# Upward products of a dense layer: high and low part of x in one product of 512 columns, with both sums left in PSUM for other engines to add

## The chip, the cores and the metric

The kernel runs on one core of one Trainium2 chip. The metric is the device time of the whole program in microseconds (us), the median of several runs. The engines are TensorE (PE, with its weight loads as PEld), VectorE (DVE), ScalarE (ACT), GpSimd (POOL) and SyncE (SP), which only issues transfers here.

## What is computed

The reference chains two transformer blocks over 256 positions of width 1024, all in float32. What the change touches are the three dense feed-forward parts:

```python
def swiglu(h, w1, w3, w2):                      # first block, D_FF = 2816
    return (jax.nn.silu(h @ w1) * (h @ w3)) @ w2
...
for l in range(DEPTH):                          # second block, two layers
    mod = c_act @ w_ada[l] + b_ada[l]
    ...
    h = rmsnorm(x, norm_mlp_g[l]) * (1.0 + sc2) + sh2
    x = x + g2 * (jnp.square(jax.nn.relu(h @ w_up[l])) @ w_down[l])   # w_up: 1024 x 4096
```

## The kernel before

**Split operands.** A float32 product is made of three products of rounded parts: with w = w_hi + w_lo and x = x_hi + x_lo it adds w_hi·x_hi, w_hi·x_lo and w_lo·x_hi (function `product`, lines 563 to 565). x is split once per stage. The weights stream from memory in slots of 128x2048 into a ring of six buffers; each slot is two halves of 128x1024. For every half ACT rounds it into `w_hi` (line 2321) and DVE subtracts to get `w_lo` (line 1416). There are three buffers of `w_hi`/`w_lo`, so a half can be rounded only when PE has finished the half three before it.

**Order.** All engines run written-out, in-order programs. `split_to(m)` on ACT and on DVE works off the splits up to half m; `reach(n)` is the number of halves that can be split once PE has finished n of them, which is n + 3 here. What stands behind a `split_to` waits in the same queue.

**Upward and downward products.** A step j makes 256 (of 2816 or 4096) hidden features. An upward half is 8 steps of k, each with three matmuls of 256 columns (`feature_tile`): w_hi, w_lo stand as weights and x moves. Two upward halves of one slot share one PSUM bank (256 columns each). The FFN needs two such slots in a step (w1, "gate", and w3, "up"), so four upward halves, called u0 to u3 below; the MLP needs one slot, u0 and u1. The downward product of the step before follows, two halves d0 and d1, each 12 matmuls of 512 columns. PE thus runs u0, u1, (u2, u3,) d0, d1 and again u0. The FFN has J1 = 11 steps, each of the two MLPs J2 = 16.

**The hidden values.** When the upward halves of step j are done, ACT applies Silu or Relu from PSUM into `ff` (line 2497), DVE multiplies (line 1663), rounds to `h_hi` (1427) and subtracts to `h_lo` (1428). The downward product of step j waits for that, one step of upward products later; after the last step there is no such upward work between, only one downward half and the first third of a group.

**Folds.** The slots of w_ada are streamed between the slots of the FFN and of the first MLP (layer 0), 24 in each. DVE takes each in whole, in two instructions (lines 1394 and 1402; the first 16 by the one, the last 8 by the other), in `split_to` right ahead of the first half of the slot that it is hung to. By `stream_order` the FFN has a fold ahead of each slot from its fifth to its last, except the slots 8, 13, 18, 23 and 28 (slot 0 is the first); the first MLP has one ahead of each from slot 4 to 31 except 8, 14, 20 and 26. The second MLP has none. In the FFN the first slot of step j is slot 3j-1, in the MLP 2j-1, so a fold stands ahead of u0 in 7 steps of the FFN (slots 5, 11, 14, 17, 20, 26, 29) and in 13 steps of the first MLP (all odd slots from 5 to 29).

## Time and profile before

| | before |
|---|---|
| median of 3 runs | 1919.96 us (1919.83 to 1922.27) |
| the profiled execution, first to last instruction | 1919.5 us |
| PE / PEld busy | 97% / 84% |
| DVE / ACT busy | 80% / 63% |
| granted TensorE clock, mean | 0.991 |
| FFN stage, 132 to 328 us | DVE 158.6 of 195.5 us busy |
| first MLP, 1395 to 1583 us | DVE 167.9 of 188.0 us busy |
| second MLP, 1728 to 1910 us | DVE 109.9 of 182.0 us busy |

The profile is one execution taken by the hardware profiler. The profiled execution's own time is its span, 1919.5 us from the first to the last instruction, 0.5 us under the median of the runs. Matmuls are pipelined, so their speed is read from the distance between two starts, not from the length of one.

### The profile page before, as it was taken

The numbers are of one execution on the slowest core, as the hardware profiler recorded it, in microseconds if no ns is written. First come the engines' busy times: TensorE is split into PE (matmuls) and PEld (weight loads), VectorE is DVE, ScalarE is ACT, GpSimd is POOL, SyncE is SP. The second block draws the span as 40 slices with busy tenths as digits, with TensorE's granted clock in tenths as the row PEclk, the third lists the DMA queues.
The fourth block names the chain that finished last, engine by engine and source line by source line (L and its number), as shares of the span: only waits on it lengthen the run. The fifth ranks groups of instructions, "written<-read, shape, count | busy, mean of one in ns | idle before, by whom it ended". The sixth has DMA issues, their size and how long they took to land.

```text
span 1919.5 us, 27067 instructions
## 1 busy us (share of the span) xinstructions
PE 1855.8 (97%) x10592; PEld 1606.9 (84%) x10592; DVE 1527.7 (80%) x2097; ACT 1200.0 (63%) x1650; POOL 46.1 (2%) x56
## 2 busy tenths in 40 slices
PE   8999999999999999999999999899999999999998
PEld 7889998788888888888888887688789988878997
DVE  5768887568999999999999999667589985756565
ACT  4544444646888888888888887567454446744443
POOL 0010000002000000000000010000000000000000
PEclk9999999999999999999999999999999999999999
DMA  8348896755999999999999999343278974315451
GB/s 317 132 165 307 329 346 245 279 203 218 420 389 377 383 377 390 369 391 375 396 368 388 367 403 380 145 154 129 69 272 332 356 278 154 129 70 187 181 192 44
DMA packets 76060, 528.37 MB, mean 275 GB/s; under 512 B 8690, under 2 KB 9074, under 8 KB 14610
## 3 DMA queue, kind: packets, MB, share of 16 engines
q1 hardware_dynamic: 69696, 504.40, 68.4%
q10 hardware_dynamic: 3060, 11.02, 1.6%
q0 software_dynamic: 3168, 11.14, 1.4%
q8 instruction: 86, 1.41, 0.3%
q14 instruction: 50, 0.41, 0.1%
HBM read 515.90 MB, written 11.01 MB: 275 GB/s over the span
## 4 chain that ended last, share of the span: by engine, by line
PE 88%; DVE 5%; ACT 3%; issue 2%; POOL 0%; DMA 0%; POOLq 0%; DVEq 0%; SPq 0%; ACTq 0%
PE ps L563 27%; PE ps L565 27%; PE ps L564 27%; PE ps L793 2%; PE ps L745 1%; DVE w_lo L1416 1%; PE ps L1015 1%; PE ps L758 1%; ACT w_hi L2321 1%; DVE arena L1402 1%; PE ps L580 0%; ACT score L2447 0%; POOL stat L2854 0%; ACT xT L2331 0%; PE ps L998 0%
## 5 line engine op out<-in xcount | busy, mean ns | idle before, releaser
L2321 ACT ACTIVATE w_hi<-ring 128x1024 fp32r<-128x1024 f32 x862 | 911.3, 1061 | 561.7 <-PE ps L565 551.9
L1416 DVE TENSOR_TENSOR w_lo<-ring,w_hi 128x1024 fp32r<-128x1024 f32 x862 | 1040.7, 1222 | 237.2 <-ACT w_hi L2321 224.2
L563 PE MATMUL ps<-w_hi,x_hi 128*128 128x512 f32 (+1 forms) x1056 | 409.5, 390 | 3.7 <-DVE x_lo L2011 1.4
L565 PE MATMUL ps<-w_hi,x_lo 128*128 128x512 f32 (+1 forms) x1056 | 399.7, 381 | 0.0
L564 PE MATMUL ps<-w_lo,x_hi 128*128 128x512 f32 (+1 forms) x1056 | 398.4, 380 | 0.0
L563 PE MATMUL ps<-x_hi,w_hi 128*128 128x256 f32 x1248 | 358.1, 287 | 8.4 <-DVE x_lo L1523 6.1
L564 PE MATMUL ps<-x_lo,w_hi 128*128 128x256 f32 x1248 | 353.7, 283 | 0.0
L565 PE MATMUL ps<-x_hi,w_lo 128*128 128x256 f32 x1248 | 353.6, 283 | 0.0
L563 PE MATMUL ps<-w_hi,h_hi 128*128 128x512 f32 x732 | 285.5, 390 | 2.7 <-DVE h_lo L1428 1.8
L564 PE MATMUL ps<-w_lo,h_hi 128*128 128x512 f32 x732 | 284.9, 389 | 0.0
L565 PE MATMUL ps<-w_hi,h_lo 128*128 128x512 f32 x732 | 284.3, 388 | 0.0
L563 PEld LDWEIGHTS ps<-x_hi,w_hi 128*128 128x128 f32 x1248 | 239.9, 192 | 14.2 <-DVE x_lo L1523 6.6
L564 PEld LDWEIGHTS ps<-x_lo,w_hi 128*128 128x128 f32 x1248 | 240.1, 192 | 1.4
L565 PEld LDWEIGHTS ps<-x_hi,w_lo 128*128 128x128 f32 x1248 | 239.9, 192 | 0.0
L563 PEld LDWEIGHTS ps<-w_hi,x_hi 128*128 128x128 f32 (+1 forms) x1056 | 192.4, 182 | 42.4 <-issue 2.5
L565 PEld LDWEIGHTS ps<-w_hi,x_lo 128*128 128x128 f32 (+1 forms) x1056 | 192.3, 182 | 40.4
L564 PEld LDWEIGHTS ps<-w_lo,x_hi 128*128 128x128 f32 (+1 forms) x1056 | 192.8, 183 | 35.9
L563 PEld LDWEIGHTS ps<-w_hi,h_hi 128*128 128x128 f32 x732 | 137.6, 188 | 31.4 <-DVE h_lo L1428 3.0
L565 PEld LDWEIGHTS ps<-w_hi,h_lo 128*128 128x128 f32 x732 | 137.4, 188 | 28.8
L564 PEld LDWEIGHTS ps<-w_lo,h_hi 128*128 128x128 f32 x732 | 137.6, 188 | 26.7
L1394 DVE CUSTOM_DVE_ANT_0 arena<-ring,arena 128x1024 f32<-128x1024 f32 x64 | 75.7, 1220 | 0.0
L2041 DVE TENSOR_TENSOR h_lo<-ps,h_hi 128x256 fp32r<-128x256 f32 x88 | 37.3, 424 | 28.0 <-ACT h_hi L2636 27.9
(297 smaller groups left out, 1283.6 us busy)
## 6 DMA issues: line engine op xcount, KB each, us to landing
ring<-in_stream SPq DMA_DIRECT2D x478, 1024.0 KB, 6.9
x_store<-arena ACTq DMA_DIRECT2D x1, 4096.0 KB, 31.6
arena<-x_store POOLq DMA_DIRECT2D x7, 512.0 KB, 8.3
y_store<-y_slots POOLq DMA_DIRECT2D x7, 512.0 KB, 8.7
con<-in_consts ACTq DMA_DIRECT2D x1, 2048.0 KB, 17.8
arena<-in_ln_rows ACTq DMA_DIRECT2D x3, 512.0 KB, 5.4
resid<-in_x SPq DMA_DIRECT2D x2, 512.0 KB, 5.1
ring<-in_stream SPq DMA_DIRECT2D x2, 512.0 KB, 8.0
```

Source lines behind the costliest of these rows:

```text
L563: pe.matmul(out_, lhs[0], rhs[0], start=start, stop=False)
L564: pe.matmul(out_, lhs[0], rhs[1], start=False, stop=False)
L565: return pe.matmul(out_, lhs[1], rhs[0], start=False, stop=stop)
L745: last = pe.matmul(at, q, k, start=True, stop=True)
L758: last = pe.transpose(ps[0:kp, 4 + n // 4, (n % 4) * P:(n % 4 + 1) * P], (score_c[:, qb] if kind == "nsac" else score[:, g % 2]) [:, u, kb ...
L793: last = pe.matmul(ps[:, mix_bank(layer, g), o * vw:(o + 1) * vw], probT[0:kp, g % 2, u * nkb + kb, :], v, start=kb == 0, stop=kb == nkb - 1)
L1015: last = pe.transpose(ps[:, 2, c:c + P], hid_rows[:, s % 2, i * P:(i + 1) * P], ident)
L1394: ins = dve.tensor_tensor_reduce(out=dots[:, i % 2, :], in0=src, in1=c_row, scale=1.0, scalar=0.0, op0=ALU.mult, op1=ALU.add, accum_out=ad ...
L1402: ins = dve.scalar_tensor_tensor(out=acc[:, part, :], in0=src, scalar=csilu[:, k:k + 1], in1=acc[:, part, :], op0=ALU.mult, op1=ALU.add)
L1416: dve.tensor_tensor(lo, ring[:, q % RING, a:a + HALF], hi.bitcast(F32), ALU.subtract)\
L2041: dve.tensor_tensor(h_lo[:, s % 2, 0:256], ps[:, 2, c:c + 256], h_hi[:, s % 2, 0:256].bitcast(F32), ALU.subtract).then_inc(moe.hidT_lo, 1)
L2321: act.activation(half_buffer(m)[0], ring[:, q % RING, a:a + HALF], ACT.Copy).then_inc(hi_ready, 1)
```

## The change

`x_hi` and `x_lo` become two halves of one tile `x_both`. An upward half now makes, for each k, one matmul of w_hi with 512 columns (x_hi and x_lo side by side) into a whole bank, and one of w_lo with x_hi, 256 columns, into the bank's first half. The low sum in the second half of the bank is a separate sum. So two banks hold what one held: ACT copies the low sums to `xT`, DVE adds them to the high sums, and ACT rounds the hidden value. The FFN's four banks are used in every step, so PE waits for the adds of the step before; the MLP alternates between two pairs. Where a tile is waited for, the splits ahead of it run to `reach(2 * done - 1)`, and the next half is split behind the tile. Everywhere else the products are as before.

```diff
-        x_hi = sb("x_hi", [P, KT, S], F32R)
-        x_lo = sb("x_lo", [P, KT, S], F32R)
+        x_both = sb("x_both", [P, 2, KT, S], F32R)
+        x_hi, x_lo = x_both[:, 0], x_both[:, 1]
...
+            def wide_tile(m, b):
+                hi, lo = half_slot(m, KT)
+                for k in range(KT):
+                    x_tile(k)
+                    pe.matmul(ps[:, b, :].rearrange("p (v s) -> p v s", v=2), hi[:, k, :], x_both[:, :, k, :],
+                              start=k == 0, stop=False)
+                    last = pe.matmul(ps[:, b, 0:S], lo[:, k, :], x_hi[:, k, :], start=False, stop=k == KT - 1)
+                last.then_inc(half_done, 1)
...
-            def up(n, banks, j, ready):
+            def gated_up(n, j):
+                for s in range(2):
+                    if j >= 1:
+                        pe.wait_ge(sums_made, 2 * (j - 1) + s + 1)
+                    for i in range(2):
+                        wide_tile(2 * (n + s) + i, 2 * s + i)
+
+            def up(n, j, ready):
                 if j >= 2:
                     pe.wait_ge(hid_ready, ready(j - 2))
-                for s, b in enumerate(banks):
-                    for i in range(2):
-                        feature_tile(2 * (n + s) + i, b, i)
+                for i in range(2):
+                    wide_tile(2 * n + i, 2 * (j % 2) + i)
...
-            def hidden(j, ready, done, paired):
-                split_to(2 * done + PAIRS)
-                dve.wait_ge(act_ready, ready(j))
+            def both_parts(out_, b):
+                parts[0] += 1
+                dve.wait_ge(part_kept, parts[0])
+                return dve.tensor_tensor(out_.rearrange("p (a s) -> p a s", a=2), ps[:, b:b + 2, 0:S],
+                                         xT[:, b:b + 2, :], ALU.add)
+
+            def hidden(j, done, paired):
                 p = j % 2
-                other = acth[:, p, :]
-                if paired:
-                    slots_done(done)
-                    other = ps[:, 2 * p + 1, :]
                 if hids[0]:
                     dve.wait_ge(hid_ready, hids[0])
-                link(dve.tensor_tensor(ff[:, 2, :], acth[:, p, :], other, ALU.mult))
-                split(h_hi[:, p, :], h_lo[:, p, :], ff[:, 2, :]).then_inc(hid_ready, 1)
+                if paired:
+                    split_to(reach(2 * (done - 1)))
+                    both_parts(acth[:, p, :], 0).then_inc(sums_made, 1)
+                    split_to(reach(2 * done - 1))
+                    both_parts(ff[:, 2, :], 2).then_inc(sums_made, 1)
+                    dve.wait_ge(sums_made, 2 * j + 2)
+                    dve.wait_ge(act_ready, j + 1)
+                    dve.tensor_tensor(acth[:, p, :], acth[:, p, :], ff[:, 2, :], ALU.mult).then_inc(hid_made, 1)
+                else:
+                    split_to(reach(2 * done - 1))
+                    link(both_parts(ff[:, 2, :], 2 * p))
+                    dve.scalar_tensor_tensor(out=acth[:, p, :], in0=ff[:, 2, :], scalar=0.0, in1=ff[:, 2, :],
+                                             op0=ALU.max, op1=ALU.mult).then_inc(hid_made, 1)
+                split_to(reach(2 * done))
                 hids[0] += 1
+                dve.wait_ge(hid_hi, hids[0])
+                dve.tensor_tensor(h_lo[:, p, :], acth[:, p, :], h_hi[:, p, :].bitcast(F32), ALU.subtract)\
+                    .then_inc(hid_ready, 1)
...
-            def activations(j, done, func, paired):
-                slots_done(done)
-                act.activation(acth[:, j % 2, :], ps[:, (2 if paired else 1) * (j % 2), :], func)\
-                    .then_inc(act_ready, 1)
+            def hidden_hi(j, done, paired):
+                def keep_part(b, end):
+                    split_to(reach(2 * end - 1))
+                    act.wait_ge(half_done, 2 * end)
+                    act.activation(xT[:, b:b + 2, :], ps[:, b:b + 2, S:2 * S], ACT.Copy).then_inc(part_kept, 1)
+                    split_to(reach(2 * end))
+                if paired:
+                    keep_part(0, done - 1)
+                    act.wait_ge(sums_made, 2 * j + 1)
+                    act.activation(acth[:, j % 2, :], acth[:, j % 2, :], ACT.Silu).then_inc(act_ready, 1)
+                keep_part(2 if paired else 2 * (j % 2), done)
+                hids[0] += 1
+                act.wait_ge(hid_made, hids[0])
+                act.activation(h_hi[:, j % 2, :], acth[:, j % 2, :], ACT.Copy).then_inc(hid_hi, 1)
```

What DVE has in its queue around the hidden values of one step of the first MLP, before. The two ISA rows on `ring` are one fold (its short rows only read out a sum), 1416 is a weight split:

```order
1664 L1394 ISA arena,ada_sums<-ring,arena 128x1024 [waits folded,landed2]
1665 L1394 ISA ada_sums 128x1
1666 L1394 ISA arena,ada_sums<-ring,arena 128x1024 [waits folded]
1667 L1394 ISA ada_sums 128x1
1668 L1416 TENSOR_TENSOR w_lo<-ring,w_hi 128x1024 [waits hi_ready]
1669 L1663 TENSOR_TENSOR ff<-ff 128x512 [waits hid_ready,act_ready]
1670 L1427 CAST h_hi<-ff 128x512 [waits dve_step]
1671 L1428 TENSOR_TENSOR h_lo<-ff,h_hi 128x512 [waits dve_step]
1672 L1416 TENSOR_TENSOR w_lo<-ring,w_hi 128x1024 [waits hi_ready]
```

The same place in the changed kernel (1437 is the weight split, 1415 the fold, 1678 the add of the two sums, 1698 Relu and square, 1703 the low part):

```order
1707 L1437 TENSOR_TENSOR w_lo<-ring,w_hi 128x1024 [waits hi_ready] x2
1708 L1678 TENSOR_TENSOR ff<-ps,xT 128x512 [waits part_kept]
1709 L1698 SCALAR_TENSOR_TENSOR ff<-ff 128x512 [waits dve_step]
1710 L1415 ISA arena,ada_sums<-ring,arena 128x1024 [waits folded,landed0]
1711 L1415 ISA ada_sums 128x1
1712 L1415 ISA arena,ada_sums<-ring,arena 128x1024 [waits folded]
1713 L1415 ISA ada_sums 128x1
1714 L1437 TENSOR_TENSOR w_lo<-ring,w_hi 128x1024 [waits hi_ready]
1715 L1703 TENSOR_TENSOR h_lo<-ff,h_hi 128x512 [waits hid_hi]
1716 L1437 TENSOR_TENSOR w_lo<-ring,w_hi 128x1024 [waits hi_ready,hid_ready]
```

The fold and the split of the next step's u0 stood ahead of the hidden values; now they stand behind the add and the square, which themselves wait for PE to finish u1 and for ACT's copy.

On ACT in the FFN, before, the queue of one step (2321 rounds a weight half, 2497 is Silu):

```order
84 L2321 ACTIVATE w_hi<-ring 128x1024 [waits half_done,landed1] x2
85 L2321 ACTIVATE w_hi<-ring 128x1024 [waits half_done,landed3] x2
86 L2321 ACTIVATE w_hi<-ring 128x1024 [waits half_done,landed4]
87 L2497 ACTIVATE ff<-ps 128x512 [waits half_done]
88 L2321 ACTIVATE w_hi<-ring 128x1024 [waits half_done,landed4]
```

And one step of the changed kernel there (2359 rounds a weight half, 2540 copies a low sum, 2546 is Silu, 2550 rounds the hidden value):

```order
93 L2540 ACTIVATE xT<-ps 128x512 [waits half_done]
94 L2359 ACTIVATE w_hi<-ring 128x1024 [waits half_done,landed3]
95 L2546 ACTIVATE ff<-ff 128x512 [waits sums_made]
96 L2359 ACTIVATE w_hi<-ring 128x1024 [waits half_done,landed3]
97 L2540 ACTIVATE xT<-ps 128x512 [waits half_done]
98 L2359 ACTIVATE w_hi<-ring 128x1024 [waits half_done,landed4]
99 L2550 ACTIVATE h_hi<-ff 128x512 [waits hid_made]
100 L2359 ACTIVATE w_hi<-ring 128x1024 [waits half_done,landed4]
```

Silu no longer waits for PE alone but for DVE's first add (`sums_made`), and the rounding of d1, the next 2359 row, is queued behind it.

## Rows read from the trace of the kernel before

**Rows 1.** The page, part 1 (busy us, share) and part 4 (the chain).
```profile
PE 1855.8 (97%) x10592; PEld 1606.9 (84%) x10592; DVE 1527.7 (80%) x2097; ACT 1200.0 (63%) x1650; POOL 46.1 (2%) x56
...
PE 88%; DVE 5%; ACT 3%; issue 2%; POOL 0%; DMA 0%; POOLq 0%; DVEq 0%; SPq 0%; ACTq 0%
```
**Rows 2.** Windows of FFN, first and second MLP: us, busy (count) by engine.
```profile
132.50:328.00 195.50, 193.40 (x1346) 180.03 (x1347) 158.63 (x191) 83.96 (x95) 0.00 (x0) 1.00 0.81 310
1395.00:1583.00 188.00, 185.22 (x1170) 166.64 (x1170) 167.91 (x214) 85.07 (x101) 1.10 (x2) 1.00 0.83 316
1728.00:1910.00 182.00, 180.05 (x1154) 163.81 (x1153) 109.93 (x125) 77.85 (x90) 0.00 (x0) 1.00 0.43 154
```
**Rows 3.** Waits of PE: total us, times, longest; then DVE's in the first MLP.
```profile
PE ps L563 <- DVE h_lo L1428: 1.8, 3, 0.8
...
DVE w_lo L1416 <- ACT w_hi L2321: 15.2, 19, 1.7
```
**Rows 4.** Timeline of PE, first MLP: u1's end, d0 and d1, u0.
```profile
1519.29 0.28 PE L564 MATMUL ps<-x_lo,w_hi 128*128 128x256 f32 x1
1519.41 0.28 PE L565 MATMUL ps<-x_hi,w_lo 128*128 128x256 f32 x1
1519.53 0.40 PE L563 MATMUL ps<-w_hi,h_hi 128*128 128x512 f32 x1
1519.76 0.40 PE L564 MATMUL ps<-w_lo,h_hi 128*128 128x512 f32 x1
...
1524.77 0.39 PE L565 MATMUL ps<-w_hi,h_lo 128*128 128x512 f32 x1
1525.00 0.28 PE L563 MATMUL ps<-x_hi,w_hi 128*128 128x256 f32 x1
```
**Rows 5.** Timeline of DVE, first MLP, one step with two folds.
```profile
1519.14 2.48 DVE L1402 SCALAR_TENSOR_TENSOR arena<-ring,csilu,arena 128x1024 f32<-128x1024 f32 x2
1521.54 1.22 DVE L1416 TENSOR_TENSOR w_lo<-ring,w_hi 128x1024 fp32r<-128x1024 f32 x1
1522.67 0.69 DVE L1663 TENSOR_TENSOR ff<-ff 128x512 f32<-128x512 f32 x1
1523.39 0.43 DVE L1427 CAST h_hi<-ff 128x512 fp32r<-128x512 f32 x1
1523.86 0.69 DVE L1428 TENSOR_TENSOR h_lo<-ff,h_hi 128x512 fp32r<-128x512 f32 x1
1524.46 1.22 DVE L1416 TENSOR_TENSOR w_lo<-ring,w_hi 128x1024 fp32r<-128x1024 f32 x1
1530.37 2.48 DVE L1402 SCALAR_TENSOR_TENSOR arena<-ring,csilu,arena 128x1024 f32<-128x1024 f32 x2
```
**Rows 6.** Timeline of DVE in the FFN: product from PSUM; then a fold.
```profile
148.61 0.69 DVE L1663 TENSOR_TENSOR ff<-ff,ps 128x512 f32<-128x512 f32 x1 [0.68 <-ACT ff L2497]
149.33 0.43 DVE L1427 CAST h_hi<-ff 128x512 fp32r<-128x512 f32 x1
...
151.64 1.22 DVE L1394 CUSTOM_DVE_ANT_0 arena<-ring,arena 128x1024 f32<-128x1024 f32 x1
...
153.93 1.23 DVE L1416 TENSOR_TENSOR w_lo<-ring,w_hi 128x1024 fp32r<-128x1024 f32 x1
```
**Rows 7.** Timeline of ACT in the FFN: Silu, the instruction behind it, a rounding.
```profile
147.98 0.60 ACT L2497 ACTIVATE ff<-ps 128x512 f32<-128x512 f32 x1
148.47 1.05 ACT L2540 ACTIVATE arena<-arena 128x1024 f32<-128x1024 f32 x1
...
158.09 0.58 ACT L2497 ACTIVATE ff<-ps 128x512 f32<-128x512 f32 x1
```
**Rows 8.** Timeline around the first MLP's last upward half and the wait behind it.
```profile
1564.41 0.40 PE L563 MATMUL ps<-w_hi,h_hi 128*128 128x512 f32 x1
1564.67 1.06 ACT L2321 ACTIVATE w_hi<-ring 128x1024 fp32r<-128x1024 f32 x1 [1.82 <-PE ps L565]
1568.29 0.39 PE L565 MATMUL ps<-w_hi,h_lo 128*128 128x512 f32 x1
1568.74 0.69 DVE L1428 TENSOR_TENSOR h_lo<-ff,h_hi 128x512 fp32r<-128x512 f32 x1
1569.48 0.50 PE L563 MATMUL ps<-w_hi,h_hi 128*128 128x512 f32 x1 [0.80 <-DVE h_lo L1428]
1569.82 0.40 PE L564 MATMUL ps<-w_lo,h_hi 128*128 128x512 f32 x1
```
**Rows 9.** Timeline of DVE in the second MLP: what it waits there.
```profile
1812.82 0.69 DVE L1663 TENSOR_TENSOR ff<-ff 128x512 f32<-128x512 f32 x1
1814.60 1.22 DVE L1416 TENSOR_TENSOR w_lo<-ring,w_hi 128x1024 fp32r<-128x1024 f32 x1
1817.14 1.23 DVE L1416 TENSOR_TENSOR w_lo<-ring,w_hi 128x1024 fp32r<-128x1024 f32 x1 [1.31 <-ACT w_hi L2321]
1820.02 1.23 DVE L1416 TENSOR_TENSOR w_lo<-ring,w_hi 128x1024 fp32r<-128x1024 f32 x1 [1.65 <-ACT w_hi L2321]
```

More of the change, by code:

```diff
@@ L415, in build @@
         act_ready = sem("act_ready")
+        part_kept = sem("part_kept")
+        sums_made = sem("sums_made")
+        hid_made = sem("hid_made")
+        hid_hi = sem("hid_hi")
         hid_ready = sem("hid_ready")
@@ L826, in swiglu @@
                     if j < J1:
-                        up(n, [2 * (j % 2), 2 * (j % 2) + 1], j, ready)
+                        gated_up(n, j)
                         n += 2
@@ L1362, in _ @@
                     if j < J2:
-                        up(n, [j % 2], j, ready)
+                        up(n, j, ready)
                         n += 1
@@ L1649, in _ @@
             hids = [0]
-            def hidden(j, ready, done, paired):
-                split_to(2 * done + PAIRS)
-                dve.wait_ge(act_ready, ready(j))
+            parts = [0]
+            def both_parts(out_, b):
[4 more added lines that the diff above has]
+            def hidden(j, done, paired):
                 p = j % 2
-                other = acth[:, p, :]
-                if paired:
-                    slots_done(done)
-                    other = ps[:, 2 * p + 1, :]
                 if hids[0]:
                     dve.wait_ge(hid_ready, hids[0])
-                link(dve.tensor_tensor(ff[:, 2, :], acth[:, p, :], other, ALU.mult))
-                split(h_hi[:, p, :], h_lo[:, p, :], ff[:, 2, :]).then_inc(hid_ready, 1)
+                if paired:
[12 more added lines that the diff above has]
+                split_to(reach(2 * done))
                 hids[0] += 1
+                dve.wait_ge(hid_hi, hids[0])
+                dve.tensor_tensor(h_lo[:, p, :], acth[:, p, :], h_hi[:, p, :].bitcast(F32), ALU.subtract)\
+                    .then_inc(hid_ready, 1)
             def keep_heads(gain):
@@ L1868, in _ @@
             for j in range(J1):
-                hidden(j, lambda j: j + 1, W_FFN0 + swiglu_up(j) + 1, True)
+                hidden(j, W_FFN0 + swiglu_up(j) + 1, True)
             def split_ple(layer):
@@ L2288, in _ @@
                 norm(7 + 2 * l, modg[:, 1, :], ada[:, 16:24], next_half=2 * (n0 + B_MLP))
-                base = J1 + l * J2
                 for j in range(J2):
-                    hidden(j, lambda j: base + j + 1, n0 + B_MLP + mlp_up(j) + 1, False)
+                    hidden(j, n0 + B_MLP + mlp_up(j) + 1, False)
                 if l == 1:
@@ L2491, in two_heads @@
                                ps[:, b, :].rearrange("p (t f s) -> p t f s", t=2, f=2), ACT.Copy).then_inc(catT_hi, 1)
-            def activations(j, done, func, paired):
-                slots_done(done)
-                act.activation(acth[:, j % 2, :], ps[:, (2 if paired else 1) * (j % 2), :], func)\
-                    .then_inc(act_ready, 1)
+            hids = [0]
+            def hidden_hi(j, done, paired):
[12 more added lines that the diff above has]
+                act.activation(h_hi[:, j % 2, :], acth[:, j % 2, :], ACT.Copy).then_inc(hid_hi, 1)
             act.wait_ge(resid1_in, 16)
@@ L2543, in _ @@
             for j in range(J1):
-                activations(j, W_FFN0 + swiglu_up(j) + 1, ACT.Silu, True)
+                hidden_hi(j, W_FFN0 + swiglu_up(j) + 1, True)
                 if j == 0:
@@ L2837, in _ @@
                 for j in range(J2):
-                    activations(j, n0 + B_MLP + mlp_up(j) + 1, ACT.Relu, False)
+                    hidden_hi(j, n0 + B_MLP + mlp_up(j) + 1, False)
                     if (l, j) == (0, 0):
```

## The prediction

> **What bounds the kernel now.** The page comes first: PE is busy 97% of the span, and 88% of the chain that ends last is PE's own work; only 5% is DVE and 3% ACT [rows 1]. A shorter PE program is therefore time won, and anything that makes PE wait is time lost. Next the windows of the three stages that the change touches: DVE is busy 158.6 of 195.5 us in the FFN, 167.9 of 188.0 in the first MLP, 109.9 of 182.0 in the second [rows 2]. The first two carry the folds. PE still hardly waits: of the downward products only the last of each stage wait, 1.8 us in three times. Where DVE waits in the first MLP it is for ACT's rounding, 15.2 us in 19 times [rows 3]. In a step with two folds it does not wait at all: one such step is 1530.37 - 1519.14 = 11.23 us of DVE work end to end [rows 5], and PE's step is as long (two upward halves of 24 x 0.12 us and 5.47 us of downward ones make 11.23, distances as in rows 4). So DVE has time on the average and none in such a step, and what matters is in which order it does its work.
>
> **What PE saves.** Two starts of 256-column matmuls lie 0.12 us apart, of 512-column ones 0.23 (18 of them plus the first six in 1525.00 - 1519.53 = 5.47 us make 0.228) [rows 4]. At the full clock, 256 columns are 106.7 ns and 512 are 213.3, so each matmul carries about 13.3 ns besides its columns. The change keeps the columns and takes away one matmul in three: 11 x 4 x 8 in the FFN and 2 x 16 x 2 x 8 in the MLPs, 352 + 512 = 864. At 13.3 ns that is 11.5 us: 4.7, 3.4 and 3.4. An upward half becomes 2.77 us instead of 2.88. Bounds: no row shows a 512-column product that follows one of 256 and reads from two places. The first ones of d0 behind 256 columns stand 0.23 to 0.235 apart; at 0.235 only 4 us are saved, and if the two pieces cost what two products cost, nothing. I take 0.227, since the columns come one by one in either form and the pieces are 256 long. The Trainium skill, TensorE: Matmul & The Clock Gate, section "Wait — 56ns, not 53.3ns?", gives a fixed 2.5 ns per warm matmul. By it the saving would be 2.2 us, 9 less; the distances of rows 4 do not agree with it, since they show five times as much.
>
> **What moves.** I count from the start of the matmul behind u1 in an MLP (time 0); PE then runs d0 and d1 and wants the next u0 at 5.47 [rows 4]. Before, DVE did the fold and the split of that u0 while PE was still in u1, and then the hidden values [rows 5]. Now they stand behind the tile. The path:
> - ACT starts 0.26 after the matmul (1564.67 - 1564.41) [rows 8], copies 512 columns in 0.58 (as Silu from PSUM) and DVE starts 0.03 later (147.98 + 0.60 to 148.61) [rows 6, 7]: 0.87.
> - The add, then the square behind it, linked: 0.72 as from 148.61 to 149.33 [rows 6]: 1.59. The square takes the place of the product, 0.60 to 0.64 until the next start (0.60 is the low part's, 1523.86 to 1524.46) [rows 5]: 2.21.
> - The fold: 2.29 in its first form (151.64 to 153.93) [rows 6], 2.40 in its second (1519.14 to 1521.54) [rows 5]: 4.50 or 4.61.
> - The split of u0, 1.23, and 0.05 to PE (1568.74 + 0.69 to 1569.48) [rows 5, 8]: 5.78 or 5.89.
>
> PE waits 0.31 or 0.42. The first matmul behind a wait also loads its weights in the open: the second starts 0.34 behind it instead of 0.23 [rows 8]. That makes 0.43 or 0.54 per step with a fold ahead of u0. Without that fold the split is ready at 3.5 and nothing waits. The cover of this fold was u1; it is gone by the order of the queue, not by load.
>
> **First MLP.** 13 steps have the fold ahead of u0, 9 in the first form and 4 in the second: 9 x 0.43 + 4 x 0.54 = 6.0 us. After a wait DVE goes on with low part, u1's split, a fold, d0's and d1's splits: 1.14 + 0.72 + 1.14 + 2.4 + 1.14 + 1.14 = 7.7, from 1.28 before PE's start on, so it is free at 6.4 and the next copy arrives at 5.54 + 0.87 = 6.4. Lateness does not add up. At the end PE has only one downward half and a third of a group between u1 and the last hidden values. Before, they came so that the matmul started 1569.48 - 1564.41 = 5.07 after time 0 [rows 8]. Now: 2.21, fold 4.61, a split 5.75, the low part until 6.44, start 6.5: 1.4 more. Sum: -3.4 + 6.0 + 1.4 = **+4.0**.
>
> **FFN.** Here the path of u2 and u3 is entangled with that of u0 and u1. After u1 (time 0): copy at 0.26, rounding of d0 at 0.75 (the start behind Silu is 0.49 later) [rows 7] until 1.81, its split on DVE at 1.84, the add at 2.98 until 3.66, Silu at 3.7, behind it the rounding of d1 at 4.2 until 5.26, its split at 5.3, and the second add at 6.43. u3 ends at 5.54 and its copy would allow 6.41. So an undisturbed step has the same path as the MLP, 0.43. But a fold ahead of d0 pushes d0's split by 0.17, and in a step that began with a wait and has folds ahead of u2 and d0 as well DVE reaches it 1.2 late (low part, u1, fold, u2, u3, fold: 1.14 + 0.72 + 1.14 + 2.29 + 1.14 + 1.14 + 2.29 = 9.86 from -1.28 on, so 8.58, against 5.54 + 1.84 = 7.38). The seven steps then cost about 0.6, 0.9, 0.4, 1.6, 0.6, 1.2 and 0.55, 5.9 us; the late ones are those behind slots 14 to 16 and behind 8 and 23, where the late DVE got half back. The last step is a late one too, and it has a fold behind it: second add at 2.3 after u3, product 3.0, fold 3.6 to 6.0, split, low part until 7.85, start 7.9 against 5.07: +2.8. Sum: -4.7 + 5.9 + 2.8 = **+4.0**.
>
> **Second MLP.** No folds; DVE idles 1.3 to 1.65 us before each split [rows 9]. u0's split is ready at 3.5 of 5.47. -3.4, and the last hidden values come 0.2 earlier: **-3.6**.
>
> Costed at nothing: PE's wait for the adds (banks 0 and 1 are added 3.7 after u1 and wanted 11 after it), ACT's extra copies (84 to 85 us busy of 188 to 195 [rows 2]), the second PSUM bank, later fold releases for the stream (six slots of ring). They cost if DVE is some 5 us late.
>
> The sum is 4.0 + 4.0 - 3.6 = +4.4 us on the profiled 1919.5, which lies 0.5 under the median 1919.96: **1924.4**.
>
> **The rivals.** What the measurement can tell from no change is 0.2%, 3.8 us.
> 1. The waits come as above: 1920.5 to 1928.5 by errors of 0.2 us in each of 20 waits. Chance 0.50, of it 0.42 over 1923.8.
> 2. The waits between steps are about half as long (6 instead of 11.9), because add, square or copy are a little quicker than the rows they are taken from: -1.6, 1918.4. For it speaks that the margin is only 0.31 us; against it that each link is a measured one. 0.22, no measurable change.
> 3. The other side: they vanish. The point from which this decides is a path under 5.47 us, 0.31 less than worked out; then only the two ends stay: -11.5 + 2.8 + 1.4 - 0.2 = -7.5, 1912.4. 0.13, faster.
> 4. The wide product costs more than 0.227: at 0.235 a step of k costs 0.355 and 7.2 us less is saved, 1931.6; as two products, 11.5 less, 1935.9. Nothing in the trace excludes it. 0.15, slower. Read as a mechanism of this kernel, a cost per matmul far under 13.3 ns (the rest being of each piece of columns) ends between these two and has 0.03 of that chance; the 2.5 ns of the Trainium skill, TensorE: Matmul & The Clock Gate, would give 1933.7.
>
> Together faster 0.13, same 0.30 (0.22 and 0.08), slower 0.57. The range is from just under rival 3 to the first form of rival 4: 1911.5 to 1932; the likeliest case alone is 1920.5 to 1928.5.
>
> **What would show it.** In the profile after: 864 fewer PE rows and 0.347 us per k; PE waits for the w_lo split in the list of waits, about 20 times with 0.3 to 1.5 us, all in FFN and first MLP and none in the second, whose step shrinks from 11.22 to 11.0; on DVE the row after the square is a fold, then u0's split, and PE's start 0.05 behind that. The waits at the two ends grow to about 2.3 and 3.6. It would be wrong if the wide products stand more than 0.23 apart, if DVE's add or square is far from 0.7, or if PE waits in steps without a fold ahead of u0.

## The result, and the profile after

| | before | after |
|---|---|---|
| median of 4 runs | 1920.69 us (1919.83 to 1922.27) | 1934.47 us (1932.77 to 1938.19) |
| ratio after / before | | 1.0072 (95%: 1.006 to 1.0084) |
| span of the profiled execution | 1919.5 us | 1935.3 us |

The change makes the kernel 13.8 us slower. The forecast was 1924.4 us, slower by 4.4, in a range that ended at 1932.

The profiled execution is the slowest of the four. The other three have spans of 1930.0, 1931.8 and 1931.9 us; why becomes clear below. The page of after, part 1 and the chain's first line:

```profile
PE 1861.0 (96%) x9728; PEld 1563.8 (81%) x9728; DVE 1544.0 (80%) x2108; ACT 1237.0 (64%) x1715; POOL 45.3 (2%) x56
...
PE 79%; DVE 12%; ACT 4%; issue 4%; POOL 0%; DMA 0%; POOLq 0%; DVEq 0%; SPq 0%; ACTq 0%
```

PE has 864 matmuls fewer, and yet DVE's part of the chain has grown from 5% to 12% [rows 1]: the end of the program now hangs on DVE in more places. The waits of PE say where. Columns: engine and line <- releaser: us in total, times, longest; first over the whole span, then FFN alone, then the first MLP alone.

```profile
PE ps L632 <- DVE w_lo L1437: 6.6, 20, 1.3
PE ps L567 <- DVE h_lo L1703: 5.6, 2, 3.4
...
PE ps L632 <- DVE w_lo L1437: 3.8, 7, 1.3
PE ps L567 <- DVE h_lo L1703: 3.4, 1, 3.4
...
PE ps L632 <- DVE w_lo L1437: 2.8, 13, 0.3
PE ps L567 <- DVE h_lo L1703: 2.2, 1, 2.2
```

Before, PE waited for no weight split there. Now it does so 20 times, 7 in the FFN and 13 in the first MLP, in exactly the steps with a fold ahead of u0, and it waits for the hidden values at the two ends, 3.4 and 2.2 us. The windows of the stages, each a little longer than those of [rows 2], and of four short stretches (columns: us, busy us and count of PE, PEld, DVE, ACT and POOL, granted clock, DMA share, GB/s):

```profile
132.50:330.00 197.50, 188.91 (x973) 158.32 (x972) 164.97 (x199) 95.02 (x118) 0.00 (x0) 0.98 0.82 306
1395.00:1590.00 195.00, 187.34 (x929) 153.81 (x928) 173.09 (x215) 95.46 (x117) 1.12 (x2) 1.00 0.81 300
1735.00:1920.00 185.00, 182.35 (x921) 153.51 (x920) 118.08 (x134) 93.08 (x115) 1.10 (x2) 1.00 0.44 155
...
54.00:57.40 3.40, 3.40 (x18) 3.18 (x16) 2.12 (x10) 1.65 (x8) 0.00 (x0) 0.50 0.59 202
320.20:327.00 6.80, 5.35 (x13) 4.18 (x14) 2.53 (x3) 0.00 (x0) 0.00 (x0) 0.50 0.87 308
368.00:371.40 3.40, 3.29 (x12) 2.54 (x11) 3.40 (x7) 2.87 (x8) 0.00 (x0) 0.50 0.33 76
1378.40:1381.80 3.40, 3.40 (x13) 2.72 (x13) 2.10 (x3) 1.53 (x2) 0.00 (x0) 0.50 0.07 27
```

In the last four the granted clock is 0.50, that is 1.2 GHz. None of the four has a counterpart before: in the same pieces of the program the profile of before shows 1.00. The one at 320.20 lies in the FFN's end. PE works 5.35 us in it at half speed, so it costs 2.7 us. The other three lie where no code is changed, and each costs up to 1.7 us.

To see where the 15.8 us of the two spans come from, I take the start of DVE's first addition to the residual behind each stage as a mark, and compare how much each stretch between marks has grown (worked out from unrounded times, so the last digit can differ by one from the marks shown):

| stretch | before, mark at | after, mark at | growth |
|---|---|---|---|
| up to the mark ahead of the FFN (has 54.0) | 122.96 | 124.51 | +1.55 |
| FFN (has 320.2) | 317.91 | 327.24 | **+7.78** |
| up to the next mark (has 368.0) | 428.95 | 439.36 | +1.09 |
| up to the first MLP (has 1378.4) | 1384.54 | 1397.06 | +2.11 |
| first MLP | 1573.90 | 1591.67 | **+5.24** |
| between the MLPs | 1720.20 | 1738.08 | +0.11 |
| second MLP | 1908.89 | 1924.63 | **-2.13** |

The three changed stages grow by 10.9 us. The other 4.9 us of this execution stand in the stretches with the three short falls of the clock. The other three executions were not traced. Their spans are only 10.5 to 12.4 us over 1919.5, so, if the three stages grew there as they did here, they hold one such stretch more than before at the most. The median time grew by about 1 us more than their spans (the time is 2.4 to 2.9 us over the span after, 1.7 to 1.8 in before's later runs); the trace shows nothing outside the span. By the same reckoning the traced execution of before, with its span of 1919.5 us, stands for a time of some 1921.3 us, an estimate, and not for one under the median.

### The profile page after: what moved, and what is told of

It reads as the page before. It is cut to its first block, busy times and chain, and to the rows that moved or that the text cites. A ratio compares the mean times of both kernels' runs of the same rounds, so it can differ in the third digit from the quotient of the medians.

```text
span 1935.3 us, 25436 instructions
## 1 busy us (share of the span) xinstructions
PE 1861.0 (96%) x9728; PEld 1563.8 (81%) x9728; DVE 1544.0 (80%) x2108; ACT 1237.0 (64%) x1715; POOL 45.3 (2%) x56
## 4 chain that ended last, share of the span: by engine, by line
PE 79%; DVE 12%; ACT 4%; issue 4%; POOL 0%; DMA 0%; POOLq 0%; DVEq 0%; SPq 0%; ACTq 0%
PE ps L567 20%; PE ps L569 20%; PE ps L568 20%; PE ps L632 7%; PE ps L634 4%; DVE w_lo L1437 3%; DVE arena L1415 2%; PE ps L807 2%; ACT w_hi L2359 2%; DVE arena L1423 1%; PE ps L759 1%; DVE ff L1678 1%; PE ps L1036 1%; PE ps L772 1%; PE ps L584 1%
## 5 line engine op out<-in xcount | busy, mean ns | idle before, releaser
L567 PE MATMUL ps<-w_hi,x_both 128*128 128x512 f32 (+1 forms) x1056 | 410.5, 391 | 3.1 <-DVE x_both L2050 1.4
L569 PE MATMUL ps<-w_hi,x_both 128*128 128x512 f32 (+1 forms) x1056 | 400.2, 381 | 0.0
L568 PE MATMUL ps<-w_lo,x_both 128*128 128x512 f32 (+1 forms) x1056 | 399.3, 380 | 0.0
L632 PE MATMUL ps<-x_both,w_hi 128*128 128x512 f32 x864 | 308.6, 400 | 11.6 <-DVE w_lo L1437 6.6
L634 PE MATMUL ps<-x_both,w_lo 128*128 128x256 f32 x864 | 242.1, 280 | 0.0
L567 PEld LDWEIGHTS ps<-w_hi,x_both 128*128 128x128 f32 (+1 forms) x1056 | 193.0, 183 | 42.3 <-issue 2.1
L569 PEld LDWEIGHTS ps<-w_hi,x_both 128*128 128x128 f32 (+1 forms) x1056 | 192.8, 183 | 40.6
L568 PEld LDWEIGHTS ps<-w_lo,x_both 128*128 128x128 f32 (+1 forms) x1056 | 193.3, 183 | 36.0
L632 PEld LDWEIGHTS ps<-x_both,w_hi 128*128 128x128 f32 x864 | 162.2, 188 | 60.7 <-issue 16.9
L634 PEld LDWEIGHTS ps<-x_both,w_lo 128*128 128x128 f32 x864 | 163.1, 189 | 0.7
L567 PE MATMUL ps<-x_both,w_hi 128*128 128x256 f32 x384 | 113.4, 295 | 3.3 <-DVE x_both L1544 2.9
L568 PE MATMUL ps<-x_both,w_hi 128*128 128x256 f32 x384 | 110.0, 286 | 0.0
L569 PE MATMUL ps<-x_both,w_lo 128*128 128x256 f32 x384 | 109.6, 286 | 0.0
L567 PEld LDWEIGHTS ps<-x_both,w_hi 128*128 128x128 f32 x384 | 75.1, 196 | 5.6 <-DVE x_both L1544 3.2
## 6 DMA issues: line engine op xcount, KB each, us to landing
con<-in_consts ACTq DMA_DIRECT2D x1, 2048.0 KB, 17.5
```

Of the source, the lines that this page charges most:

```text
L567: pe.matmul(out_, lhs[0], rhs[0], start=start, stop=False)
L568: pe.matmul(out_, lhs[0], rhs[1], start=False, stop=False)
L569: return pe.matmul(out_, lhs[1], rhs[0], start=False, stop=stop)
L632: pe.matmul(ps[:, b, :].rearrange("p (v s) -> p v s", v=2), hi[:, k, :], x_both[:, :, k, :], start=k == 0, stop=False)
L634: last = pe.matmul(ps[:, b, 0:S], lo[:, k, :], x_hi[:, k, :], start=False, stop=k == KT - 1)
```

## The step with a fold, the end of the FFN, and the pair

Timeline of after, one step of the first MLP (start, length, engine, line, operation, operands, [idle before it <- releaser]):

```profile
1500.10 0.40 PE L567 MATMUL ps<-w_hi,h_hi 128*128 128x512 f32 x1
...
1500.30 0.60 ACT L2540 ACTIVATE xT<-ps 128x512 f32<-128x512 f32 x1 [1.71 <-PE ps L634]
1500.93 0.69 DVE L1678 TENSOR_TENSOR ff<-ps,xT 128x512 f32<-128x512 f32 x1 [0.28 <-ACT xT L2540]
1501.66 0.69 DVE L1698 SCALAR_TENSOR_TENSOR ff<-ff 128x512 f32<-128x512 f32 x1
1502.27 1.22 DVE L1415 CUSTOM_DVE_ANT_0 arena<-ring,arena 128x1024 f32<-128x1024 f32 x1
...
1503.41 1.22 DVE L1415 CUSTOM_DVE_ANT_0 arena<-ring,arena 128x1024 f32<-128x1024 f32 x1
...
1504.56 1.22 DVE L1437 TENSOR_TENSOR w_lo<-ring,w_hi 128x1024 fp32r<-128x1024 f32 x1
1505.70 0.68 DVE L1703 TENSOR_TENSOR h_lo<-ff,h_hi 128x512 fp32r<-128x512 f32 x1
...
1505.92 0.47 PE L632 MATMUL ps<-x_both,w_hi 128*128 128x512 f32 x1 [0.20 <-DVE w_lo L1437]
1506.23 0.28 PE L634 MATMUL ps<-x_both,w_lo 128*128 128x256 f32 x1
...
1517.38 0.47 PE L632 MATMUL ps<-x_both,w_hi 128*128 128x512 f32 x1 [0.20 <-DVE w_lo L1437]
```

Read from 1500.10, the matmul behind u1: copy at 0.20, add at 0.83, square at 1.56, the fold at 2.17, the split of u0 at 4.46, PE at 5.82. The forecast had 0.26, 0.87, 1.59, 2.21, 4.50 and 5.78. PE, which would be ready for u0 at 5.47, stands still, and the next step begins 11.46 us later, as DVE's path sets it.

The end of the FFN, same view:

```profile
317.38 2.47 DVE L1423 SCALAR_TENSOR_TENSOR arena<-ring,csilu,arena 128x1024 f32<-128x1024 f32 x2
...
319.77 1.22 DVE L1437 TENSOR_TENSOR w_lo<-ring,w_hi 128x1024 fp32r<-128x1024 f32 x1
320.91 0.69 DVE L1703 TENSOR_TENSOR h_lo<-ff,h_hi 128x512 fp32r<-128x512 f32 x1
...
321.65 0.79 PE L567 MATMUL ps<-w_hi,h_hi 128*128 128x512 f32 x1 [3.45 <-DVE h_lo L1703]
322.24 0.63 PE L568 MATMUL ps<-w_lo,h_hi 128*128 128x512 f32 x1
322.67 0.63 PE L569 MATMUL ps<-w_hi,h_lo 128*128 128x512 f32 x1
```

The last hidden values wait behind a fold and a split, and PE waits 3.45 us for them. Behind that wait the starts lie 0.43 us apart instead of 0.23: this is the half clock of the window at 320.20.

And the pair of products in the second MLP, where PE waits for nothing:

```profile
1855.01 0.39 PE L632 MATMUL ps<-x_both,w_hi 128*128 128x512 f32 x1
1855.24 0.28 PE L634 MATMUL ps<-x_both,w_lo 128*128 128x256 f32 x1
1855.35 0.40 PE L632 MATMUL ps<-x_both,w_hi 128*128 128x512 f32 x1
1855.59 0.28 PE L634 MATMUL ps<-x_both,w_lo 128*128 128x256 f32 x1
...
1860.65 0.40 PE L567 MATMUL ps<-w_hi,h_hi 128*128 128x512 f32 x1
```

The first wide product takes 0.227. The ones behind a product of 256 take 0.233 to 0.241, so that the 16 wide ones have a mean of 0.236; the narrow ones take 0.116 instead of the 0.12 of before. The 16 pairs of u0 and u1 need 1860.65 - 1855.01 = 5.64 us, where the forecast had 5.55 and the 48 products of before take 5.75. So 0.11 us is saved in 16 pairs, some 6 us in the 54 times that the program has them, and not 11.5.

## The experiments

The theory behind the first ones: three things make up the growth, (a) the fold that DVE now takes between the square and the split of u0, (b) the half clock behind the long wait at the FFN's end, and (c) the pair, 0.3525 us instead of 0.347. The rivals were that DVE is simply overloaded by the adds, whatever the order, and that the pair's cost lies in the wide product itself. Growth by stage is always by the marks above, against the profile of before, in the order FFN, first MLP, second MLP. The medians are against a before of 1921.1 to 1921.3 us in these comparisons.

**1. The fold ahead of the tile's wait.** DVE folds the slot that is due before it waits for the tile, and no longer behind the square:

```diff
                 else:
                     split_to(reach(2 * done - 1))
+                    fold_ahead(reach(2 * done - 1))
                     link(both_parts(ff[:, 2, :], 2 * p))
```

`fold_ahead(m)` does the folds that `split_to` would do ahead of half m; in the FFN it stands between the two adds.

> The changed kernel with one difference: the fold of the slot that comes next is done by DVE before the tile is waited for (in the FFN between the two adds, in the MLPs ahead of the add), and only the split of the half stays behind it. Theory (order of DVE's queue): the 20 waits of PE for a w_lo split in FFN and first MLP (6.6 us idle, some 0.1 more each) go, the two waits for the last hidden values shrink from 3.4 and 2.2 us to about 1, and the 6.8 us at 1.2 GHz that follow the first of them go too: 15 to 17 us less than the changed kernel, near 1918. Rival (DVE has simply too much to do in these steps, and the waits only move to another half): PE waits for w_lo as long as before in total, less than 3 us gained, about 1932.

Measured: 1916.99 us (1915.9 to 1919.85, 11 runs), ratio to before 0.9979 (0.997 to 0.9988). The list of waits has no row of PE for a weight split any more. Timeline of a step of the first MLP:

```profile
1493.97 1.22 DVE L1415 CUSTOM_DVE_ANT_0 arena<-ring,arena 128x1024 f32<-128x1024 f32 x1
...
1494.17 0.40 PE L567 MATMUL ps<-w_hi,h_hi 128*128 128x512 f32 x1
...
1495.12 1.22 DVE L1415 CUSTOM_DVE_ANT_0 arena<-ring,arena 128x1024 f32<-128x1024 f32 x1
...
1496.26 0.69 DVE L1686 TENSOR_TENSOR ff<-ps,xT 128x512 f32<-128x512 f32 x1
1496.99 0.69 DVE L1710 SCALAR_TENSOR_TENSOR ff<-ff 128x512 f32<-128x512 f32 x1
1497.60 1.22 DVE L1445 TENSOR_TENSOR w_lo<-ring,w_hi 128x1024 fp32r<-128x1024 f32 x1
...
1499.63 0.39 PE L632 MATMUL ps<-x_both,w_hi 128*128 128x512 f32 x1
```

The same instructions in another order: the fold starts before u1 ends and still ends after the copy is there, so the add starts 2.09 us behind the matmul at 1494.17, 1.26 later than in the changed kernel; but the split of u0 now starts 3.43 us behind it instead of 4.46, and PE starts u0 5.46 behind it without a wait. Growth by stage is now -2.31, -1.02 and -2.12. This refutes an overload of DVE and bears out (a) and (b) together: 17.5 us for one call, moved ahead of a wait. It says nothing on (c).

**2. The early fold in the FFN's last step alone.**

```diff
+                    if j == J1 - 1:
+                        fold_ahead(reach(2 * done - 1))
```

> The changed kernel with the early fold in the FFN's last step alone. Theory (PE's 3.4 us without work there make the granted clock fall to 1.2 GHz for 6.8 us): the wait shrinks to 1 to 1.5 us, the stretch at half clock behind it is gone, 2.2 and 3.4 make 5.6 us less. Rival (the clock falls at that place whatever the length of the wait): 2.2 us less and the stretch stays.

Measured: 1929.18 us (1927.86 to 1931.94, 5 runs), 5.3 under the changed kernel. The FFN grows by 3.26 instead of 7.78. PE's wait at its end is 1.4 instead of 3.4 us, and the clock stays up. The window over the same piece of the program:

```profile
319.00:326.00 7.00, 7.00 (x31) 5.45 (x30) 2.85 (x5) 2.03 (x3) 0.00 (x0) 1.00 0.77 312
```

Compare it with 320.20:327.00 above: 31 matmuls in 7 us instead of 13 in 6.8. Of the 4.5 us, 2.0 are the wait and about 2.7 the clock. So the wait of 3.45 us cost nearly twice its length in the traced execution, and one of 1.4 cost its length.

The length of the wait is not all that decides it, as the other kernels with this late fold show. At the FFN's end experiments 3 and 5 wait 3.0 and 3.4 us, and the clock is down for 3.4 us behind it, half as long as in the changed kernel. At the first MLP's end PE waits 2.15 to 2.17 us in the changed kernel and in experiments 2, 3 and 5: in the first the clock stays up, in the other three it falls for 3.4 us. That fall is in this experiment's first MLP, which grows by 6.62 where the same code grew by 5.24. Windows of experiment 5 and 3 behind the FFN's end, of experiment 2 and of the changed kernel behind the first MLP's end:

```profile
321.90:325.20 3.30, 3.30 (x10) 2.56 (x9) 0.18 (x1) 0.00 (x0) 0.00 (x0) 0.50 0.93 357
322.50:325.80 3.30, 3.30 (x9) 2.56 (x8) 0.00 (x0) 0.00 (x0) 0.00 (x0) 0.50 0.96 375
1577.60:1580.90 3.30, 3.30 (x8) 2.62 (x9) 0.98 (x1) 0.00 (x0) 0.00 (x0) 0.50 0.94 355
1585.00:1592.00 7.00, 4.84 (x22) 3.90 (x22) 4.90 (x6) 0.00 (x0) 0.00 (x0) 1.00 0.96 344
```

The 2.7 us are thus what the traced execution lost. Waits of 3.0 and 3.4 us in the same place went with half clock for half as long, and what the untraced executions had there is not known.

**3. The wide product as two of 256 columns**, everything else as in the changed kernel:

```diff
-                    pe.matmul(ps[:, b, :].rearrange("p (v s) -> p v s", v=2), hi[:, k, :], x_both[:, :, k, :],
-                              start=k == 0, stop=False)
+                    pe.matmul(ps[:, b, 0:S], hi[:, k, :], x_hi[:, k, :], start=k == 0, stop=False)
+                    pe.matmul(ps[:, b, S:2 * S], hi[:, k, :], x_lo[:, k, :], start=False, stop=False)
```

> The changed kernel with each product of 512 columns made as two of 256, into the same places of PSUM; queues of DVE and ACT as in the change. Theory (PE's program sets the upward halves, so the pair's 0.3532 us against 3 x 0.12 is all that the wide product gives): 864 x 0.0068 = 5.9 us, of which the steps that wait for DVE give some back through their slack: 4 to 6 us more than the changed kernel. Rival (the wide product saves the 11.5 us that were forecast, and the time was lost elsewhere): 9 to 11.5 us more.

Measured: 1937.53 us (1936.78 to 1942.95, 5 runs), 3.1 over the changed kernel and less than the 4 to 6 that were expected. Part of the gain hides in the waits, which shrink by 0.8 us with the longer upward halves, and this profile holds other falls of the clock. The clean place is the second MLP: it ends 0.34 us earlier than before, and 2.13 with the wide product. 1.8 us over 256 pairs is 0.007 us for each pair, half of the forecast 13.3 ns.

**4. The same two products with the fold first**, so that no wait covers anything (edits of 1 and 3 together).

> The kernel with the early folds, each product of 512 columns made as two of 256. It prices the wide product where PE does not wait for folds. Theory: 864 x 0.0068 = 5.9 us more than with the wide product, near 1922.5. Rival (DVE sets the steps with folds): only the second MLP and the steps without a fold lose, 2 to 3 us more, near 1919.5.

Measured: 1921.26 us (1919.45 to 1924.56, 11 runs), ratio to before 1.0001 (0.9992 to 1.001), 4.3 over experiment 1. Growth by stage: -0.36, +0.43 and -0.38, against -2.31, -1.02 and -2.12 with the wide product. The difference is 5.1 us for 864 pairs, 0.006 each; by the distances of starts (5.75 against 5.64 us over 16 pairs) it is 0.007. It is also the answer to what all the rest of the change costs when the fold is in its place: the copies, the adds, the second bank and the new order together cost nothing that can be measured, which is to say less than 2 us.

**5. Eight wide products, then eight narrow ones**, in the changed kernel (the loop over k runs once over the wide and once over the narrow products):

```diff
-                for k in range(KT):
-                    x_tile(k)
-                    pe.matmul(...wide, k)
-                    last = pe.matmul(...narrow, k)
+                for k in range(KT):
+                    x_tile(k)
+                    pe.matmul(...wide, k)
+                for k in range(KT):
+                    last = pe.matmul(...narrow, k)
```

> The changed kernel with the products of each upward half in another order: the eight of 512 columns one behind the other, then the eight of 256. In the changed kernel a pair takes 0.3532 us, where 0.227 and 0.12 make 0.347. Theory A (what costs is that 512 columns follow 256): a group of eight loses only some 0.03 us at its head, so an upward half shortens by 0.02 to 0.05 us, 108 halves: 2 to 5.5 us less than the changed kernel, and the starts of wide products settle at 0.227. Theory B (the operand read from two places costs it): all wide starts stay 0.233 or more apart and the time stays within 1 us.

Measured: 1935.49 us (1934.68 to 1936.98, 5 runs), no gain. The first half of a step did become 2.77 us and both together 5.56, as the theory of the alternation has it. But the kernel's step with a fold is set by DVE, so a shorter half only makes PE wait longer (7.2 us for weight splits instead of 6.6). At a stage's start the eight wide products ask for all of x at once (4.5 us in 8 waits for x, 3.4 in 6 with alternation): the first MLP's first four halves take 14.92 us instead of 13.28. And this profile has four short stretches at half clock that before does not have. The second MLP, which holds one of them (at 1748.6), gained only 1.30. So the distance was explained and the time not yet.

**6. Both: fold first, and grouped except in the first half of a stage**, where x is still being made:

```diff
+                g = KT if unsplit[0] is None else 1
+                for k0 in range(0, KT, g):
```

(wide products of k0 to k0 + g, then the narrow ones of the same k).

> The kernel with the early folds, and in every upward half but the first of a stage the eight products of 512 columns one behind the other, then the eight of 256 (in the first half x arrives tile by tile, and grouping made PE wait for it). Theory (alternating the widths costs 0.0065 us a pair, and without waits for DVE that shows): 105 halves by 0.04 to 0.05 us, 4 to 5 us less than with early folds alone, near 1912.5; upward halves of 2.77 to 2.79 us instead of 2.83. Rival (DVE has no slack left in the steps with two folds, so a faster PE only waits): only the second MLP gains, 1 to 1.5 us, near 1915.7.

Measured: **1912.32 us** (1910.74 to 1915.18, 5 runs), ratio to before 0.9962 (0.9948 to 0.9975). It beats both kernels. Growth by stage -4.03, -2.05 and -3.32. Rows of PE in the second MLP (x8 stands for eight matmuls in one row):

```profile
1852.82 1.98 PE L634 MATMUL ps<-x_both,w_hi 128*128 128x512 f32 x8
1854.63 1.12 PE L637 MATMUL ps<-x_both,w_lo 128*128 128x256 f32 x8
1855.58 0.63 PE L634 MATMUL ps<-x_both,w_hi 128*128 128x512 f32 x2
...
1858.38 0.40 PE L567 MATMUL ps<-w_hi,h_hi 128*128 128x512 f32 x1
```

Eight pairs in 1855.58 - 1852.82 = 2.76 us, the half that the prediction wanted. The second half of the step takes 2.79 (its wide products first stand 0.23 to 0.235 apart), so 16 pairs need 1858.38 - 1852.82 = 5.56 us against a forecast 5.55. The second MLP's -3.32 is near the forecast -3.6, which was right for this order of the products and not for the alternating one.

**7. Groups of two**, to see whether it is each change from narrow to wide that costs: experiment 6 with `g = 2`, which halves the number of such changes.

> The kernel with early folds, upward halves but the first of a stage in groups of two: two products of 512 columns, two of 256, and again. Theory (a cost for each change from 256 to 512 columns, 0.0069 us): half of what groups of eight gain, 1914.5 to 1915, and an upward half of 2.80 us. Rival (only a long run of equal widths reaches the quick distance, as d0's first six starts suggest): no gain over the alternating order, 1917.

Measured: 1914.4 us (1910.63 to 1914.77, 5 runs), ratio 0.9963 (0.9949 to 0.9976). The time alone would fit the theory, since it lies where 1914.5 to 1915 was expected; but the runs of experiments 6 and 7 overlap, and a difference of 2 us can be one or two short falls of the clock. The trace decides it. Start of u0 and of the d0 behind the step's last group:

```profile
1851.20 0.62 PE L634 MATMUL ps<-x_both,w_hi 128*128 128x512 f32 x2
...
1856.76 0.40 PE L567 MATMUL ps<-w_hi,h_hi 128*128 128x512 f32 x1
```

The 16 pairs take 5.56 us as in groups of eight, a half 2.78 and not 2.80, and the second MLP grows by -3.56, so it gains no less than with groups of eight. Half the changes did not bring half the gain but all of it. What costs is therefore not each change of width; it is something in the strict alternation of single products, and what it is these runs do not tell.

**8. The changed order on DVE alone, in the kernel before**, whose products stay three of 256:

```diff
-                split_to(2 * done + PAIRS)
+                split_to(reach(2 * done - 1))
...
-                    slots_done(done)
+                    dve.wait_ge(half_done, 2 * done)
```

(`slots_done` would do the splits first and then the same wait.)

> The kernel before with the order of the change on DVE alone: the split of the half that follows the tile, and the fold ahead of it, stand behind the hidden values instead of ahead of them. No wide product, no second bank, no adds. Theory (the order of this queue makes the waits): from the end of the last upward half 0.26 + 0.58 + 0.03 to the product, 0.72, 0.47, 0.6, fold 2.29 or 2.4, 1.28 make 6.2 to 6.3 against 5.47, so 0.75 to 0.95 with the open weight load, in 20 steps: 16 us, less 2 at the two ends whose last hidden values come earlier: 1933 to 1937. Rival (only the added copies and adds cause the waits): within 2 us of the kernel before.

Measured: 1969.91 us (1966.91 to 1970.96, 5 runs), ratio 1.0253: far more than expected. PE waits 41.7 us in 25 times for weight splits. Timeline:

```profile
1450.71 0.40 PE L563 MATMUL ps<-w_hi,h_hi 128*128 128x512 f32 x1
...
1450.97 1.06 ACT L2321 ACTIVATE w_hi<-ring 128x1024 fp32r<-128x1024 f32 x1 [1.82 <-PE ps L565]
1451.93 0.58 ACT L2497 ACTIVATE ff<-ps 128x512 f32<-128x512 f32 x1
1452.55 0.69 DVE L1663 TENSOR_TENSOR ff<-ff 128x512 f32<-128x512 f32 x1 [2.12 <-ACT ff L2497]
...
1458.00 0.36 PE L563 MATMUL ps<-x_hi,w_hi 128*128 128x256 f32 x1 [1.66 <-DVE w_lo L1416]
```

I had forgotten ACT's queue: before the change, ACT rounds a weight half ahead of Relu, and DVE's product starts 1452.55 - 1450.71 = 1.84 us behind u1, where the path that I expected had 0.87. With everything on DVE queued behind it, PE is late by that: it starts u0 7.29 us behind u1, a full microsecond more than the 6.2 to 6.3 of the expectation.

**9. The changed order on both queues, in the kernel before**: ACT, too, does Relu ahead of the rounding.

```diff
-                slots_done(done)
+                split_to(reach(2 * done - 1))
+                act.wait_ge(half_done, 2 * done)
                 act.activation(acth[:, j % 2, :], ps[:, (2 if paired else 1) * (j % 2), :], func)\
                     .then_inc(act_ready, 1)
+                split_to(reach(2 * done))
```

> The kernel before with the change's order of both queues: on DVE the fold and the split of the half that follows the tile behind the hidden values, on ACT the rounding of that half behind Relu or Silu. In the kernel that moved DVE's queue alone PE waited 41.7 us, because that rounding, 0.97 us, still stood ahead of Relu. Theory (the path from the tile to the next u0's split sets the waits): 0.26 + 0.58 + 0.03 + 0.72 + 0.47 + 0.6 + 2.29 + 1.28 make 6.2 against 5.47, 0.75 and 0.1 for the open weight load, 20 times, less 2 us at the two ends: 1934 to 1937. Rival (something else in that order costs, such as the late release of ring slots): more than 1945 still.

Measured: 1940.93 us (1940.16 to 1942.28, 4 runs), ratio 1.0101; PE waits 18.4 us in 23 times for weight splits. That is 4 us over the expected range and under the rival's 1945. The steps came as expected: one with a fold of the first form takes 12.11 us instead of 11.22 in the first MLP, 0.89 more, where 0.85 was worked out. What was wrong are the two ends, where 2 us were to be won and PE waits 2.1 us each time for a weight split. With the products of before and no low sum to add, the order of the two queues alone makes the kernel about 20 us slower. The wait of a step is 0.45 us longer than in the changed kernel (0.65 and 0.75 for the two forms of the fold, against 0.2 and 0.3). A reason by the rows, not tried by itself: here product, rounding and low part stand ahead of the fold, 0.72 + 0.47 + 0.60 = 1.79 us by [rows 5], and there only add and square, 1.34 us. Two experiments thus take the order from both sides: putting it right in the changed kernel wins 17.5 us, putting it wrong in the kernel before loses 19.7.

## Why the prediction was wrong

The direction was right and so was the mechanism of the waits; the size was not: 13.8 us instead of 4.4. Two steps failed. The term "what PE saves" was given 11.5 us and is worth about 6, and the clock behind PE's wait at the FFN's end was not in the sum, though it cost 2.7 us in the traced execution. Step by step, in the prediction's order:

- **What PE saves** (11.5 us). This is the term that was mis-sized most. "I take 0.227" was the wrong choice for the wide product; the row that the prediction itself named as the bound, 0.235, is what came, and wide products more than 0.23 apart were its own first sign of being wrong. The 16 pairs take 5.64 us, where 5.55 was wanted and before took 5.75: some 6 us are saved and 5.5 of the 11.5 are not. (By the bound 7.2 would have been lost; it is less because the narrow products became quicker, 0.116 instead of 0.12.) The total that 0.227 gives, 5.55, comes when the products are grouped (5.56, experiment 6), not when they alternate; whether the reason given for it, that the columns come one by one in either form, is the right one is not shown. Rival 4 was this case in its first form; with the 5.5 us it would alone have given 1929.9. The Trainium skill, TensorE: Matmul & The Clock Gate, section "Wait — 56ns, not 53.3ns?", gives a fixed cost of 2.5 ns per warm matmul, by which 2.2 us would have been saved in all. The measured saving of a wide product over two narrow ones is about 7 ns alternating (5.75 against 5.64 us for 16), and 12 ns when grouped (5.75 against 5.56). So neither that figure nor the 13.3 ns of the prediction is what alternating products show.
- **The path on DVE.** Right link by link: 5.82 us measured, 5.78 worked out, and the step 11.46 as it follows from them. The 20 waits came in the steps named, 0.2 to 0.3 us each in the first MLP; that they came at all on a margin of 0.31 us is no luck, since each link of the path was off by 0.08 us or less. Between steps they cost 10.5 us, where the sum had 11.9. In the first MLP PE starts u0 5.83 us behind the start of d0 in nine steps and 5.92 in four, instead of 5.47, which is 5.0, and the exposed loads add 0.6; the same reading of the seven steps of the FFN gives 4.9. The single terms in the FFN were right to some 0.6 us.
- **The two ends.** +2.8 and +1.4 were forecast. With the pairs, the waits between steps and the clock taken off, the growths leave 2.7 and 1.4. The waits in the profile are 3.4 and 2.2, where about 3.6 and 2.3 were named.
- **The clock behind the FFN's end.** This step failed, too: it was not in the sum at all. The prediction priced a wait of PE at its length and at one exposed weight load. PE's 3.45 us of standing still are followed by 5.35 us of work at 1.2 GHz, 2.7 us more. The trace of before had shown such stretches (its mean clock is 0.991; it has four of 6.8 us, near 439, 1241, 1347 and 1681), and I did not ask what PE did ahead of them. PE's longest wait at the ones near 1347 and 1681 is 1.6 us, so the length of one wait would not have been enough to tell.
- **Second MLP.** -3.6 was forecast, -2.13 came, and the pairs, 1.6 us less saved here, explain it.
- **Costed at nothing**: the copies, adds and the second bank. Right within 2 us, by experiment 4, and no list of waits has PE waiting for the adds.

The sum for the three stages: 4.4 + 5.5 (pairs) + 2.7 (clock) - 1.4 (waits between steps) - 0.1 (ends) = 11.1, and the marks give 10.9. The profiled execution has 4.9 us more in stretches without changed code, by three short stretches at half clock. What of this belongs to the change is open: of the kernels here, some with the late fold have such stretches near 368 and 1378 (the changed kernel, experiment 3) or the first of them alone (experiment 8, where that place is at 378, and experiment 9), and experiments 2 and 5 have neither; no kernel with the early fold in all steps has one in either place. The one at 54 also comes in experiment 4, which is as fast as before. The same holds for the last 1 us of the median, which lies outside the span.

## What to carry to other kernels

In an in-order queue, place work that nobody waits for (a fold) ahead of the instruction that waits for a tile, so that it runs while the wait runs; behind the wait it delays everything that the tile's consumer needs next. When products of two widths add up to one sum, write them in groups of at least two of one width, not alternating, and check the first half of a stage, where the operand is still being made. Price a long wait of PE by its length and, as a range, by a slower clock behind it (nothing to 2.7 us in these kernels), and look in the trace for what PE did ahead of each such stretch.

## What was not expected of the hardware

- Behind a single 256-column product, a 512-column one takes 0.233 to 0.241 us until the next start and the 256-column one behind it 0.113 to 0.12; in a run of its own kind the wide one settles at 0.227. The pair is 0.3525 us alternating (5.64 over 16) and 0.3475 in groups of two or of eight (5.56 over 16). After some waits a half of alternating pairs ran at 0.347 as well: the upward part of a step in the first MLP's changed kernel is 5.72 us in 8 of the 13 steps that wait and 5.63 in 5, with an exposed weight load in both. I have no explanation.
- A wait of 3.45 us of PE went with a stretch of 6.8 us at half clock, which began within the wait; 5.35 us of it were work. Waits of 3.0 and 3.4 us in the same place of other kernels went with 3.4 us at half clock, which began over 1 us behind the wait. A wait of 2.15 to 2.17 us at the first MLP's end went with 3.4 us at half clock in three kernels and with none in the changed one. With a wait of 1.4 us at the FFN's end the clock stayed at 2.4 GHz.
- The clock also falls for 3.4 us in places where nothing was changed, in some executions and kernels and not in others. It moves the time of one execution by about 1.7 us each, which is why differences of 2 us were read from stages and not from times.
